# A three-block kernel: the modulation matrix read as row dot products, and six waits or orders around it changed

## The chip, the cores and the metric

The kernel runs on one core of one Trainium2 chip. The metric is the device time of one execution in microseconds (us), here the median of three runs.

## What is computed

Three transformer-like blocks, one after another, on one sequence of 1024 positions (T) with 1024 channels (D), all in float32. The parts that this change touches:

```python
# first block: gated linear recurrence in 4 heads of 128, computed in chunks
o = einsum('bhts,bhse->bhte', scores, vc) + einsum('bhtd,bhde->bhte', qc * exp(b), S)
# third block: six vectors of 1024 from each of two conditioning vectors
def ada_split(cond, w_ada, b_ada):              # w_ada: 1024 x 6144
    return jnp.split(jax.nn.silu(cond) @ w_ada + b_ada, 6, axis=-1)
sh1, sc1, g1, sh2, sc2, g2 = ada_split(c, w_ada, b_ada)
csh1, csc1, ... = ada_split(c_ctx, w_ada, b_ada)   # only csh1, csc1 are used
```

So the third block needs all 48 blocks of 128 numbers of silu(c) @ w_ada, and the first 16 of silu(c_ctx) @ w_ada. It also needs the layer norm of a context of 256 positions. Beside this each block has a mixer and a feed-forward network; the second block's network has the activation relu squared.

## The kernel before

The text calls the engines PE (TensorE, matmuls), DVE (VectorE), ACT (ScalarE), POOL (GpSimd) and SP (SyncE, which issues the transfers). The order of the work on each engine is written out by hand in one function per engine and stage, and engines wait for each other on semaphores. A float32 matrix product is made of three passes with rounded operands (`_r` tiles, a high and a low part each), so that nearly every product shows as three lines of PE in turn, as L2372, L2373, L2374. A stage ends with a barrier of all engines (`PEq L150` in the rows).

- **block1_mix** is the first block's mixer. For each of 4 heads its recurrence takes 1024 positions as 8 chunks of 128. `scores` (L405) makes a 128x128 product of keys and queries per chunk for each of several levels r, and DVE copies what the level's mask keeps (L740). Level 0 keeps, in each chunk, only keys of the first 64 and queries of the last 64 positions.
- **conv_stage** is the first block's feed-forward network, worked in pairs of hidden chunks, j = 0 to 12. A pair has seven products r in the manner of Strassen (`up`, L1317 to L1319) and a sweep of 16 units (n, m) over the outputs (`down`, L1328 to L1330), whose results DVE drains into the residual (L1761). ACT's `copy` (L1493) takes a finished sum out of PSUM, so that its bank comes free; `round_t` on ACT and `low_t` on DVE make the high and low part of the products' inputs; `low_part` (L1712, L1715) makes the low parts of the next pair's weights.
- **the attention block** (around L4400 to L5020) spills the residual X; its SP function ends with two transfers of 2 MB that bring X back, and a wait for them (`x_back`).
- **pair_stage** holds the end of the second block's mixer and its feed-forward network, in pairs i = 0 to 12 again. `up_pair(i)` is seven products r = 0 to 6 of 12 matmuls each (L2372 to L2374), `down_pair(i)` 16 units (n, m) of 6 matmuls (L2380 to L2382), drained by DVE (L2836). A matmul of 512 columns follows the last after 0.2265 us, as [rows 2] stand, so a pair is 180 matmuls. The products write PSUM banks 0, 1, 0, 2, 0, 2, 0: r = 6 needs the bank of r = 4, which DVE's `add(i, "22")` (L2822) frees. After r = 6, `down_pair` makes two sweeps of 12 matmuls over part of its inputs; the second needs the low part `low_y(i, "21")` (L2826), which needs `add(i, "21")` and then three ACT steps (L2575, L2577, L2579).
- **PairSide** puts the third block's conditioning beside these pairs. In i = 0 and 1 it takes the context's layer norm: parts q = 2i and 2i+1 are squared, added by DVE (`add_squares`, L2033) and summed over partitions by PE (`sums`, L2020). From i = 2 on it takes the modulation: 12 groups g of four blocks of 128 outputs. Group g is worked in pair i = g + 2, group 11 in the tail behind pair 12. A group is eight pieces k (128 inputs x 512 outputs, 256 KB each). DVE's `gemv(g, k)` multiplies piece k by the conditioning of those 128 inputs and adds it to an accumulator of 128x512 (L1985; L1988 for k = 0). For the four groups with both vectors a piece takes three such instructions (512, 256, 256). `sum_up` on PE (L2000) then adds the accumulator over partitions, one matmul of one column for each block (two rows of the profile each), and `keep` on ACT copies the result out. SP loads piece k+2 when `gemv(g, k)` is done, since there are two buffers (`rows`, `masks`).
- **the tail of pair_stage**: `load_tail(e)`, `round_tail`, `low_tail(j)` (L2855) and `down_tail(n, ms, e)` handle six last hidden chunks, e = 0 to 2, beside group 11.

In pair i = 3 to 12 DVE's order is gemv 0 to 2, add "11", low_down, low_y "11", gemv 3 to 5, add "22", gemv 6, add "21", low_y "22", gemv 7, low_y "21", low_y "12", and then 16 drains with the next pair's weight sums between them. In pair 2 the eight gemvs stand among the drains.

Of the kernel before, what the change touches and what calls it, by code (L numbers as in the profile page):

```python
# [38 lines left out]
def param_spec():  # L39
# [7 lines left out]
        ("c_3", 8), ("c_ctx_3", 8), ("b_ada_3", 48), ("ln_v_g_3", 4), ("ln_v_b_3", 4),  # L47
# [13 lines left out]
class Core:  # L61


    def __init__(self, nc, ctx, inputs, out):
# [37 lines left out]
        self.ctx_norm = nc.dram_tensor("ctx_norm", (P, KT * CTX), F32, kind="Internal").ap()  # L102
        self.row_copies = nc.dram_tensor("row_copies", (2, 8, T), F32, kind="Internal").ap()
# [123 lines left out]
def block1_mix(c, prefetch):  # L227
# [55 lines left out]
    with c.stage("products", "drained", "hi_ready", "lo_ready", "w_hi", "w_lo", "pieces", "masks_set", "bounds", "exps", "chain",  # L283
# [55 lines left out]
        def _(pe):  # L339
# [74 lines left out]
            def level(h, r):  # L414
                pe.wait_ge(w_ready, 9 * h + r + 1)
                pair_free(("level", h, r))
                scores(("level", h, r), Wl[r % 2], Wl[r % 2])
# [231 lines left out]
        def _(dve):  # L649
# [81 lines left out]
            def masks(what, r):  # L731
# [6 lines left out]
                s = pair_bank(what).rearrange("p a (b n) -> p (a b) n", n=CH)  # L738
                mask = c.ident[:, :].unsqueeze(1).to_broadcast([P, NC_, P]) if r is None else c.mask(r)
# [315 lines left out]
def counted(order):  # L1055
# [8 lines left out]
                  "ctx_scaled", "ada_a", "ada_b", "gemv", "summed", "ada_kept", "side_added")  # L1064
# [11 lines left out]
def conv_stage(c, w_out, up, down, first, last, mix_scale, alpha, follow, lead):  # L1076
# [99 lines left out]
    with c.stage(*names) as (block_, *sems):  # L1176
# [233 lines left out]
        def _(act):  # L1410
# [157 lines left out]
            gelu_early(2, 1)  # L1568
            round_t(3)
            for j in range(PAIRS):  # L1570
# [3 lines left out]
                copy(j, "11", 0)  # L1574
                if j:
                    gelu(j - 1)
                    if j < END:
                        round_part(j + 1, 0)
                    round_y(j - 1)
# [80 lines left out]
        def _(dve):  # L1660
# [200 lines left out]
            for j in range(PAIRS):  # L1861
# [15 lines left out]
                if j < END:  # L1877
                    low_part(j + 1, 4)
                    low_part(j + 1, 2)
                else:  # L1880
                    low_tail(0, w0)
                add(j, "21", 5)
                if j < END:
                    low_part(j + 1, 3)
                    for n in down_halves(j - 1):
                        for m in range(KT):
                            drain(j - 1, n, m)
                            if (n, m) == (0, 2):
                                low_part(j + 1, 5)
                            if (n, m) == (0, 5):  # L1890
                                low_part(j + 1, 6)
# [39 lines left out]
class PairSide:  # L1931

    GROUPS, BOTH, PART = 12, 4, 64
    ORDER = (4, 0, 1, 2, 3) + tuple(range(5, 12))

    def __init__(self, c):
# [3 lines left out]
        self.acc = [[c.rows[:, HALF:T]], [c.rows[:, T:TT], table[:, HALF:HALF + 256]]]  # L1940
# [4 lines left out]
        self.cond = c.small[:, 0:16].rearrange("p (k s) -> p k s", s=2)  # L1945
        self.ada = c.ada[:, :].rearrange("p (j s) -> p j s", s=2)
        self.done, at = {}, 0
        for g in range(self.GROUPS):
            for k in range(KT):
                at += 3 if self.both(g) else 1  # L1950
                self.done[g, k] = at

    def both(self, p):
        return self.ORDER[p] < self.BOTH

    def columns(self, p):
        return [(v, i) for v in range(2 if self.both(p) else 1) for i in range(HALF // P)]
# [9 lines left out]
    def load(self, sp, g, k):  # L1967
        at = self.ORDER[g] * P
        w = self.c.inp["w_ada_3"][at:at + P, k * HALF:(k + 1) * HALF]
        sp.dma_start(self.part[k % 2], w).then_inc((self.s["ada_a"], self.s["ada_b"])[k % 2], 16)  # L1970

    def gemv(self, dve, g, k):

        dve.wait_ge((self.s["ada_a"], self.s["ada_b"])[k % 2], 16 * (4 * g + k // 2 + 1))
        if k == 0 and g:
            dve.wait_ge(self.s["summed"], g)
        if k:
            dve.wait_ge(self.s["gemv"], self.done[g, k - 1])
        w = self.part[k % 2]
        for v in range(2 if self.both(g) else 1):  # L1980
            by, at = self.cond[:, k, v:v + 1], 0
            for acc in self.acc[v]:
                n = acc.shape[-1]
                if k:
                    dve.scalar_tensor_tensor(out=acc, in0=w[:, at:at + n], scalar=by, in1=acc, op0=ALU.mult,  # L1985
                                             op1=ALU.add).then_inc(self.s["gemv"], 1)
                else:
                    dve.tensor_scalar(acc, w[:, at:at + n], by, None, ALU.mult).then_inc(self.s["gemv"], 1)  # L1988
                at += n

    def sum_up(self, pe, g):
        pe.wait_ge(self.s["gemv"], self.done[g, KT - 1])
        if g:
            pe.wait_ge(self.s["ada_kept"], g)
        else:
            pe.wait_ge(self.s["ctx_log"], 4)
        n = len(self.columns(g))
        for j, (v, i) in enumerate(self.columns(g)):
            src = self.acc[0][0][:, i * P:(i + 1) * P] if v == 0 else self.acc[1][i // 2][:, (i % 2) * P:(i % 2 + 1) * P]
            mm = pe.matmul(self.c.PS[:, 3, j:j + 1], src, self.c.ones[:, 0:1], start=j == 0, stop=j == n - 1, skip_group_check=True)  # L2000
        mm.then_inc(self.s["summed"], 1)

    def keep(self, act, g):
        n, at = 2 if self.both(g) else 1, 4 * self.ORDER[g]
        act.wait_ge(self.s["summed"], g + 1)
        act.activation(self.ada[:, at:at + 4, 0:n], self.c.PS[:, 3, 0:4 * n].rearrange("p (s a) -> p a s", a=4),
                       ACT.Copy).then_inc(self.s["ada_kept"], 1)
# [8 lines left out]
    def sums(self, pe, q):  # L2016
        pe.wait_ge(self.s["side_added"], self.added(q) + 2)
        pe.wait_ge(self.s["ctx_centred"], 2 * (q // 2) + 2)
        out = self.c.PS[:, 3, self.PART * (2 + q % 2):self.PART * (3 + q % 2)]
# [4205 lines left out]
```

## Time and profile before

| | before |
|---|---|
| median of 3 runs | 3537.03 us (3535.54 to 3537.22) |
| the profiled execution | 3532.54 us, span 3530.8 us |
| TensorE's mean granted clock | 0.996 of full |
| busy: PE, DVE, ACT, POOL | 98%, 71%, 41%, 9% of the span |
| packets over the span | 331 MB, 94 GB/s |

The span is what lies between the first and the last instruction of one profiled execution; 1.7 us of its time lie outside. Its time is 4.5 us under the median. In a row of the timeline, the first number is the start within the span, the second how long the row took, xN how many instructions it stands for, and the bracket how long the engine had been idle and what released it.

### The profile page before, as it was taken

The numbers are of one execution on the slowest core, as the hardware profiler recorded it, in microseconds if no ns is written. First come the engines' busy times: TensorE is split into PE (matmuls) and PEld (weight loads), VectorE is DVE, ScalarE is ACT, GpSimd is POOL, SyncE is SP. The second block draws the span as 40 slices with busy tenths as digits, with TensorE's granted clock in tenths as the row PEclk, the third lists the DMA queues.
The fourth block names the chain that finished last, engine by engine and source line by source line (L and its number), as shares of the span: only waits on it lengthen the run. The fifth ranks groups of instructions, "written<-read, shape, count | busy, mean of one in ns | idle before, by whom it ended". The sixth has DMA issues, their size and how long they took to land. (4 is left out here: it accounts for less than half of the span.)

```text
span 3530.8 us, 42878 instructions
## 1 busy us (share of the span) xinstructions
PE 3448.1 (98%) x16610; PEld 2809.7 (80%) x16610; DVE 2519.2 (71%) x3472; ACT 1455.4 (41%) x2060; POOL 311.1 (9%) x313
## 2 busy tenths in 40 slices
PE   8999999999999999999999999999999999999998
PEld 7977877888887788667877888876987878888887
DVE  5387588888887798553567877656547587888895
ACT  3344363333345422542443333335423266772123
POOL 0000012222222001221000000003010000000000
PEclk9999999999999999999999999999999999999999
DMA  3102111111112113102223222331122214667651
GB/s 134 48 1 84 60 42 54 54 54 54 52 62 96 43 59 72 37 13 101 73 72 108 96 96 96 113 125 73 60 68 67 92 39 158 258 241 293 245 198 58
DMA packets 114526, 331.24 MB, mean 94 GB/s; under 512 B 18398, under 2 KB 33374, under 8 KB 105876
## 3 DMA queue, kind: packets, MB, share of 16 engines
q1 hardware_dynamic: 114324, 328.51, 26.7%
q8 instruction: 132, 2.16, 0.2%
q14 instruction: 70, 0.57, 0.1%
HBM read 253.82 MB, written 66.13 MB: 91 GB/s over the span
## 5 line engine op out<-in xcount | busy, mean ns | idle before, releaser
L2836 DVE TENSOR_TENSOR residual<-residual,psum 128x512 f32<-128x512 f32 x224 | 149.2, 683 | 57.1 <-PE psum L2382 56.9
L2380 PE MATMUL psum<-parts_r 128*128 128x512 f32 x448 | 177.3, 396 | 3.0 <-DVE parts_r L2855 1.5
L2382 PE MATMUL psum<-parts_r 128*128 128x512 f32 x448 | 174.9, 390 | 0.0
L2381 PE MATMUL psum<-parts_r 128*128 128x512 f32 x448 | 174.8, 390 | 0.0
L3872 DVE SCALAR_TENSOR_TENSOR residual<-psum,ada,residual 128x512 f32<-128x512 f32 x192 | 137.9, 746 | 38.0 <-PE psum L3426 19.8
L1763 DVE TENSOR_TENSOR residual<-residual,psum 128x512 f32<-128x512 f32 x256 | 160.1, 680 | 0.0
L4267 DVE SCALAR_TENSOR_TENSOR mixer<-scratch,params,mixer 128x1024 f32<-128x1024 f32 x120 | 156.9, 1307 | 4.0
L1317 PE MATMUL psum<-mixer_r,parts_r 128*128 128x512 f32 x304 | 118.3, 389 | 0.7 <-ACT rows L1440 0.7
L1318 PE MATMUL psum<-gemm_input_r,parts_r 128*128 128x512 f32 x304 | 118.3, 389 | 0.0
L1319 PE MATMUL psum<-mixer_r,parts_r 128*128 128x512 f32 x304 | 118.3, 389 | 0.0
L3568 ACT ACTIVATE parts_r<-parts 128x1792 fp32r<-128x1792 f32 x24 | 40.9, 1705 | 180.3 <-DVE parts L3856 180.3
L1328 PE MATMUL psum<-pairs_r 128*128 128x512 f32 x288 | 112.8, 392 | 2.0 <-DVE residual L1761 1.8
L358 PE MATMUL psum<-gemm_input_r,weights_r 128*128 128x512 f32 x256 | 105.3, 412 | 9.4 <-DVE residual_r L675 9.3
L1330 PE MATMUL psum<-pairs_r 128*128 128x512 f32 x288 | 112.1, 389 | 0.0
L1329 PE MATMUL psum<-pairs_r 128*128 128x512 f32 x288 | 112.1, 389 | 0.0
L1500 ACT ACTIVATE pairs<-pairs,params 128x1024 f32<-128x1024 f32 x36 | 42.9, 1239 | 142.8 <-PE psum L1330 142.8
L2380 PEld LDWEIGHTS psum<-parts_r 128*128 128x128 f32 x448 | 84.4, 188 | 21.4 <-DVE residual L2836 2.9
L360 PE MATMUL psum<-gemm_input_r,weights_r 128*128 128x512 f32 x256 | 100.4, 392 | 0.0
L359 PE MATMUL psum<-residual_r,weights_r 128*128 128x512 f32 x256 | 100.3, 392 | 0.0
L4887 DVE TENSOR_REDUCE small<-psum 128x1 f32<-128x512 f32 (+2 forms) x96 | 51.7, 555 | 67.0 <-PE psum L4598 65.8
L2382 PEld LDWEIGHTS psum<-parts_r 128*128 128x128 f32 x448 | 84.4, 188 | 17.8
L2381 PEld LDWEIGHTS psum<-parts_r 128*128 128x128 f32 x448 | 84.5, 189 | 17.0 <-issue 0.2
(961 smaller groups left out, 10773.6 us busy)
## 6 DMA issues: line engine op xcount, KB each, us to landing
y_blocks<-parts_r SPq DMA_DIRECT2D x84, 512.0 KB, 3.4
parts<-in_w SPq DMA_DIRECT2D x15, 1024.0 KB, 4.7
parts<-in_w_down SPq DMA_DIRECT2D x14, 1024.0 KB, 4.9
parts<-in_w_up SPq DMA_DIRECT2D x13, 1024.0 KB, 4.9
masks<-in_w_ada SPq DMA_DIRECT2D x48, 256.0 KB, 3.1
rows<-in_w_ada SPq DMA_DIRECT2D x48, 256.0 KB, 2.9
mixer_r<-y_blocks SPq DMA_DIRECT2D x12, 1024.0 KB, 9.6
low_r<-y_blocks SPq DMA_DIRECT2D x12, 1024.0 KB, 11.7
```

Source lines behind the costliest of these rows:

```text
L1317: pe.matmul(bank, a_high(place)[:, at], high[:, k, :], start=OPENS[r] and k == 0, stop=False, skip_group_check=True)
L1318: pe.matmul(bank, a_high(place)[:, at], low[:, k, :], start=False, stop=False, skip_group_check=True)
L1319: mm = pe.matmul(bank, a_low(place)[:, at], high[:, k, :], start=False, stop=k == 3, skip_group_check=True)
L1328: pe.matmul(bank, w_high[:, at], high, start=start, stop=False, skip_group_check=True)
L1329: pe.matmul(bank, w_low[:, at], high, start=False, stop=False, skip_group_check=True)
L1763: dve.tensor_tensor(x, x, ps, ALU.add).then_inc(drained, 1)
L2380: pe.matmul(bank, w_high[:, kd, at], high[:, 2 * kd + n, :], start=start, stop=False, skip_group_check=True)
L2381: pe.matmul(bank, w_low[:, kd, at], high[:, 2 * kd + n, :], start=False, stop=False, skip_group_check=True)
L2382: return pe.matmul(bank, w_high[:, kd, at], low[:, 2 * kd + n, :], start=False, stop=stop, skip_group_check=True)
L2836: dve.tensor_tensor(x, x, ps, ALU.add).then_inc(drained, 1)
L3872: dve.scalar_tensor_tensor(out=x, in0=ps, scalar=gate(m), in1=x, op0=ALU.mult, op1=ALU.add).then_inc(drained, 1)
L4267: dve.scalar_tensor_tensor(out=out, in0=U[:, j:j + T], scalar=w, in1=out, op0=ALU.mult, op1=ALU.add).then_inc(taps, 1)
```

## The change

Ten edits, in the kernel's order:

1. **Level 0 as a rectangle** (block1_mix): PE makes only the 64x64 part of each chunk that the mask keeps, and DVE copies it with a plain copy.
2. **copy(0, "11")** stands ahead of `round_t(3)` on ACT instead of behind it (conv_stage).
3. **low_part at j = 0** (conv_stage): three of five low parts move from before the drains to among them.
4. **x_back**: the attention stage no longer waits for X; DVE waits for it in pair_stage ahead of its first `mix_drain`.
5. **Context sums** in pair_stage, i = 0 and 1: `add_squares(q+1)` stands two units earlier, the next pair's `low_sums` one later.
6. **Modulation**: w_ada is laid out transposed. A piece is now one block of 128 outputs by 512 inputs; the first half of the inputs for all 48 blocks comes first, then the second half. One DVE instruction, `tensor_tensor_reduce`, multiplies a piece by a row of 512 silu values that is the same on all partitions and sums along the row into one column of `ada`, going on from what is there in the second half. Each waits for the one before. Where both vectors are wanted it is three instructions, and these pieces now alternate with single ones: groups 1 to 4 and 7 to 10 (pairs 3 to 6 and 9 to 12) have four of each kind, in place of four groups with eight.
7. `sum_up` and `keep` are gone.
8. **Conditions**: silu is taken of 16x128 numbers, stored to HBM, and read back as rows spread over all partitions, once for each half.
9. **Tail**: `low_tail(2)` and `(3)` stand ahead of gemv 4 to 7; `down_tail` takes all m at once for each e.
10. The context's normed values are loaded only when the last tail slab has landed.

```diff
 (level 0)
+                for i in range(NC_):
+                    keys, queries = ch(Wl[0], i)[:, 0:CH // 2], ch(Wl[0], i)[:, CH // 2:CH]
+                    mm = pe.matmul(chunk_of(("level", h, r), i)[0:CH // 2, CH // 2:CH], keys, queries, ...)
+                if r == 0:
+                    dve.tensor_copy(far, s[0:CH // 2, :, CH // 2:CH]).then_inc(masked, 1)
+                    return
 (conv_stage, ACT)
+            copy(0, "11", 0)
             round_t(3)
 (conv_stage, DVE)
+                        lows = {(0, 1): 4, (0, 3): 2, (0, 5): 3, (0, 6): 5, (0, 7): 6}
 (PairSide)
-    ORDER = (4, 0, 1, 2, 3) + tuple(range(5, 12))
+    ORDER = tuple(range(32, 40)) + tuple(b for j in range(16) for b in (j, 16 + j)) + tuple(range(40, 48))
+        dve.wait_ge(self.s["gemv"], at)
+        dve.tensor_tensor_reduce(out=self.c.PS[:, 3, :] if kept else w[:, j * n:(j + 1) * n],
+                                 in0=w[:, j * n:(j + 1) * n], in1=by, scale=1.0,
+                                 scalar=out if half or j else 0.0, op0=ALU.mult, op1=ALU.add, accum_out=out)
-                        elif side is not None and (n, m) == (1 if i == 2 else 0, 6):
-                            side.sum_up(pe, i - 2)
-                side.keep(act, i - 2)
 (pair_stage, SP)
+                sp.wait_ge(*tail_landed[2 * EARLY - 2])
+                sp.wait_ge(*tail_landed[2 * EARLY - 1])
                 sp.dma_start(c.PW[:, 8:10, :], c.ctx_norm...)
 (pair_stage, DVE)
-                        if i < END and (n, m) == (1, 3):
+                        if i < END and (n, m) == (1, 4 if side is not None and i < 2 else 3):
                             low_sums(i + 1)
-                        if contexts and (n, m) == (1, 4):
+                        if contexts and (n, m) == (1, 2):
                             side.add_squares(dve, q + 1)
 (attention stage, SP)
-            sp.wait_ge(x_back, 32)
```

The order on DVE in pair 3 between its fourth product's add and its low parts, before: gemv 5 (three instructions), add "22", gemv 6 (three), add "21", low_y "22".

```order
L1985 SCALAR_TENSOR_TENSOR rows<-masks,small,rows 128x512
L1985 SCALAR_TENSOR_TENSOR rows<-masks,small,rows 128x256
L1985 SCALAR_TENSOR_TENSOR masks<-masks,small 128x256
L2822 TENSOR_TENSOR parts<-parts,psum 128x512
L2826 TENSOR_TENSOR parts_r<-parts,parts_r 128x512
```

The same place of the change, where a dot product stands as two rows, ISA with its elements and ISA 128x1, the read-out of its sum: gemv 5 (single), add "22", gemv 6 (both), add "21", low_y "22".

```order
L2020 ISA rows,ada<-rows 128x512
L2020 ISA ada 128x1
L2833 TENSOR_TENSOR parts<-parts,psum 128x512
L2020 ISA psum,ada<-masks,rows 128x512
L2020 ISA ada 128x1
L2020 ISA masks,ada<-masks,rows 128x256
L2020 ISA ada 128x1
L2020 ISA masks,ada<-masks,ada 128x256
L2020 ISA ada 128x1
L2833 TENSOR_TENSOR parts<-parts,psum 128x512
L2837 TENSOR_TENSOR parts_r<-parts,parts_r 128x512
```

So ahead of add "22" three instructions became one with a read-out, and ahead of add "21" three became three with read-outs.

The order on DVE in pair 0 from unit (1, 0) on, before (L2033 is `add_squares`, L2808 `low_sums`, L2836 a drain):

```order
L2836 TENSOR_TENSOR residual<-residual,psum 128x512
L2033 TENSOR_REDUCE rows<-rows 128x64
L2836 TENSOR_TENSOR residual<-residual,psum 128x512
L2804 TENSOR_TENSOR parts_r<-parts,parts_r 128x1024
L2836 TENSOR_TENSOR residual<-residual,psum 128x512 x2
L2808 TENSOR_TENSOR parts_r<-parts,parts_r 128x2560
L2836 TENSOR_TENSOR residual<-residual,psum 128x512
L2033 TENSOR_REDUCE rows<-rows 128x64
```

and of the change, whose lines are L2847, L2050, L2815 and L2819 for the same four:

```order
L2847 TENSOR_TENSOR residual<-residual,psum 128x512
L2050 TENSOR_REDUCE rows<-rows 128x64
L2847 TENSOR_TENSOR residual<-residual,psum 128x512
L2815 TENSOR_TENSOR parts_r<-parts,parts_r 128x1024
L2847 TENSOR_TENSOR residual<-residual,psum 128x512
L2050 TENSOR_REDUCE rows<-rows 128x64
L2847 TENSOR_TENSOR residual<-residual,psum 128x512 x2
L2819 TENSOR_TENSOR parts_r<-parts,parts_r 128x2560
```

The second reduction now stands ahead of the long `low_sums` instead of behind it.

The order on DVE in conv_stage at j = 0, before (L1712 and L1715 are `low_part`, L1727 an add, L1761 a drain):

```order
L1712 TENSOR_TENSOR parts_r<-rows,parts_r 128x1024
L1715 TENSOR_TENSOR parts_r<-parts,parts_r 128x512 x2
L1727 TENSOR_TENSOR pairs<-pairs,psum 128x512
L1715 TENSOR_TENSOR parts_r<-masks,parts_r 128x512
L1761 SCALAR_TENSOR_TENSOR residual<-residual,psum 128x512 x3
```

and of the change (L1725, L1728, L1740 and L1774 for the same):

```order
L1725 TENSOR_TENSOR parts_r<-rows,parts_r 128x1024
L1740 TENSOR_TENSOR pairs<-pairs,psum 128x512
L1774 SCALAR_TENSOR_TENSOR residual<-residual,psum 128x512 x2
L1728 TENSOR_TENSOR parts_r<-parts,parts_r 128x512
L1774 SCALAR_TENSOR_TENSOR residual<-residual,psum 128x512 x2
L1728 TENSOR_TENSOR parts_r<-parts,parts_r 128x512
```

The first drains now stand behind one short add, and the low parts between drains.

## Rows read from the trace of the kernel before

**Rows 1.** The page, busy time of each engine.

```profile
PE 3448.1 (98%) x16610; PEld 2809.7 (80%) x16610; DVE 2519.2 (71%) x3472; ACT 1455.4 (41%) x2060; POOL 311.1 (9%) x313
```

**Rows 2.** Timeline of PE in pair 5.

```profile
2010.38 0.50 PE L2372 MATMUL psum<-mixer_r,parts_r 128*128 128x512 f32 x1 [0.89 <-DVE parts L2822]
2010.71 0.40 PE L2373 MATMUL psum<-low_r,parts_r 128*128 128x512 f32 x1
...
2022.75 1.39 PE L2000 MATMUL psum<-ones,rows 128*128 128x1 f32 x12
...
2024.45 0.48 PE L2380 MATMUL psum<-parts_r 128*128 128x512 f32 x1
```

**Rows 3.** Groups by line on PE, pairs 3 to 6 (busy, mean ns | idle before).

```profile
L2372 PE MATMUL psum<-mixer_r,parts_r 128*128 128x512 f32 x75 | 29.7, 395 | 3.6 <-DVE parts L2822 3.6
```

**Rows 4.** Groups by line and shape on DVE.

```profile
L1985 DVE SCALAR_TENSOR_TENSOR rows<-rows,small 128x512 f32<-128x512 f32 x48 | 35.9, 749 | 19.7 <-DMA rows<-in_w_ada 18.3
...
L1985 DVE SCALAR_TENSOR_TENSOR rows<-rows,small 128x256 f32<-128x256 f32 x16 | 7.6, 478 | 0.0
...
L2072 DVE TENSOR_TENSOR ada<-ada,params 128x32 f32<-128x32 f32 x1 | 0.2, 186 | 0.0
...
L702 DVE TENSOR_TENSOR_SCAN mixer<-scratch 128x1024 f32<-128x1024 f32 x4 | 8.8, 2272 | 0.7 <-issue 0.7
...
L740 DVE COPY_PREDICATED norm_b<-masks,psum 128x1024 f32<-128x1024 int32 x28 | 36.5, 1303 | 4.2 <-PE psum L405 4.1
...
L4904 DVE COPY gemm_input<-psum 64x512 f32<-64x512 f32 x15 | 10.2, 682 | 0.2
```

**Rows 5.** Timeline of DVE in pair 5.

```profile
1998.97 0.75 DVE L1985 SCALAR_TENSOR_TENSOR rows<-masks,small,rows 128x512 f32<-128x512 f32 x1 [2.52 <-DMA masks<-in_w_ada]
...
2003.83 0.74 DVE L1985 SCALAR_TENSOR_TENSOR rows<-rows,small 128x512 f32<-128x512 f32 x1
...
2005.47 0.75 DVE L1985 SCALAR_TENSOR_TENSOR rows<-masks,small,rows 128x512 f32<-128x512 f32 x1
...
2008.18 0.75 DVE L1985 SCALAR_TENSOR_TENSOR rows<-rows,small 128x512 f32<-128x512 f32 x1 [1.17 <-DMA rows<-in_w_ada]
...
2009.64 0.68 DVE L2822 TENSOR_TENSOR parts<-parts,psum 128x512 f32<-128x512 f32 x1
...
2011.69 0.68 DVE L2822 TENSOR_TENSOR parts<-parts,psum 128x512 f32<-128x512 f32 x1
...
2014.41 0.69 DVE L2826 TENSOR_TENSOR parts_r<-parts,parts_r 128x512 fp32r<-128x512 f32 x1
```

**Rows 6.** Timeline of PE, whole span, rows with a wait.

```profile
185.15 2.05 PE L405 MATMUL psum<-scratch 128*128 128x128 f32 x16 [0.16 <-DVE scratch L729]
...
522.29 0.47 PE L1317 MATMUL psum<-low_r,parts_r 128*128 128x512 f32 x1 [1.81 <-ACT pairs L1493]
...
540.66 0.50 PE L1328 MATMUL psum<-pairs_r 128*128 128x512 f32 x1 [1.81 <-DVE residual L1761]
...
1606.71 0.47 PE L2326 MATMUL psum<-mixer_r,pairs_r 128*128 128x512 f32 x1 [2.67 <-PEq L150]
...
1813.51 0.43 PE L2020 MATMUL psum<-rows,ones_d 128*128 128x64 f32 x2 [1.89 <-DVE rows L2033]
...
1857.64 0.47 PE L2020 MATMUL psum<-rows,ones_d 128*128 128x64 f32 x2 [1.85 <-DVE rows L2033]
...
1903.77 0.50 PE L2380 MATMUL psum<-parts_r 128*128 128x512 f32 x1 [0.89 <-DVE residual L2836]
...
2341.14 0.50 PE L2380 MATMUL psum<-gemm_input_r,low_r 128*128 128x512 f32 x1 [0.83 <-DVE mid_r L2855]
...
2353.20 0.50 PE L2380 MATMUL psum<-parts_r 128*128 128x512 f32 x1 [1.46 <-DVE parts_r L2855]
...
2411.86 0.67 PE L943 MATMUL psum<-mixer,ones_d 128*128 128x512 f32 x1 [1.06 <-PEq L150]
```

**Rows 7.** Transfers issued from 2338 to 2352 us, median us to landing.

```profile
pairs<-ctx_norm SPq DMA_DIRECT2D x1, 1024.0 KB, 11.1
```

More of the change, by code:

```diff
@@ L1949, in __init__, with chunk, both @@
             for k in range(KT):
-                at += 3 if self.both(g) else 1
+                at += 3 if self.both(g, k) else 1
                 self.done[g, k] = at
[L1953 to L1957, printed above, removed]
+    def chunk(self, g, k):
+        half, at = divmod(KT * g + k, self.BLOCKS)
+        return half, self.ORDER[at]
+    def both(self, g, k):
+        return self.chunk(g, k)[1] < self.BOTH
     def load_part(self, sp, q, j):
@@ L1972, in gemv @@
     def gemv(self, dve, g, k):
+        half, block = self.chunk(g, k)
         dve.wait_ge((self.s["ada_a"], self.s["ada_b"])[k % 2], 16 * (4 * g + k // 2 + 1))
[L1975 to L2007, printed above, removed]
+        if (KT * g + k) % self.BLOCKS == 0:
+            dve.wait_ge(self.s["cond_moved"], 32 + 48 * (half + 1))
+        w, at = self.part[k % 2], self.done[g, k] - (3 if self.both(g, k) else 1)
@@ new lines, in gemv @@
+        for v in range(2 if self.both(g, k) else 1):
+            out = self.ada[:, block, v:v + 1]
+            for j, by in enumerate(self.by[v]):
+                n = by.shape[-1]
+                if at:
+                    dve.wait_ge(self.s["gemv"], at)
+                at += 1
+                kept = v == 0 and self.both(g, k)
+                dve.tensor_tensor_reduce(out=self.c.PS[:, 3, :] if kept else w[:, j * n:(j + 1) * n], in0=w[:, j * n:(j + 1) * n], in1=by, scale=1.0,
+                                         scalar=out if half or j else 0.0, op0=ALU.mult, op1=ALU.add,
+                                         accum_out=out).then_inc(self.s["gemv"], 1)
@@ L2477, in _ @@
                 down_pair(i)
-            if side is not None:
-                for e in TAIL:
-                    down_tail(0, range(0, 7), e)
-                    if e == 1:
-                        side.sum_up(pe, END - 1)
-                pe.wait_ge(s["ada_kept"], END)
-                for e in TAIL:
-                    down_tail(0, range(7, KT), e)
-            else:
-                for e in TAIL:
-                    down_tail(0, range(KT), e)
+            for e in TAIL:
+                down_tail(0, range(KT), e)
             if follow is None:
@@ L2940, in _ @@
                 low_t(r)
-            if side is not None:
-                dve.wait_ge(s["cond_ready"], 2)
             for i in range(PAIRS):
@@ L2993, in _ @@
                     side.scale(dve, q + 1)
-            for j in (2, 3):
-                low_tail(j)
-                if side is not None:
-                    for k in (2 * j, 2 * j + 1):
-                        side.gemv(dve, END - 1, k)
+            low_tail(2)
+            low_tail(3)
+            if side is not None:
+                for k in range(4, 8):
+                    side.gemv(dve, END - 1, k)
             low_tail(4)
```

89 lines of the change are left out of this document (59 added, 30 removed).

## Prediction, made before the changed kernel ran

> **What bounds the kernel now.** I read the page first. PE is busy for 98% of the span, DVE for 71% [rows 1]. The reader is to see that only two things can shorten this kernel: fewer rows on PE, or fewer waits of PE. DVE has time over in the mean, but where PE waits it is nearly always for DVE. So the next view was PE's timeline, every row with a bracket. PE is not busy for 3530.8 - 3448.1 = 82.7 us in all, spread over some eighty places, so each edit must be costed at its own place.
>
> What a wait costs is more than its bracket. In pair 5 the row of r = 6 has 0.89 in its bracket, but it starts 1.05 us later than the rhythm of 0.2265, and the row after it follows after 0.33 instead of 0.23 [rows 2]. So I add 0.16 to every bracket, and 0.1 for the slow start: 0.26 in all.
>
> **The modulation in pairs 3 to 12.** A pair's 180 matmuls take 180 x 0.2265 = 40.77 us. The sixteen rows of `sum_up` in a pair with both vectors start at 2022.75 and the next unit at 2024.45 [rows 2], which with a slow start is 1.80; by half, 0.90 where one vector is wanted. Four pairs have 1.80 and six have 0.90 (the tail is costed below): 12.6 us of PE rows that go. In the four pairs with both, r = 6 also waits for add "22", 3.6 us of brackets in all [rows 3], 4.6 with 4 x 0.26. If nothing took their place, 17.2 us would be won here.
>
> What takes their place is DVE's price of a dot product. No row of this trace has one. A multiply-add of 128x512 takes 0.749, one of 256 columns 0.478; a tiny operation takes 0.186 [rows 4]. Each dot product is an instruction over the piece, then a read-out of the sum, and each waits for the one before. The low bound is that the read-out hides: 0.75 and 0.48. Above it: 0.69, a plain copy's or product's time, plus 0.19 is 0.88 for 512 columns, and (0.42 + 0.19) 0.61 for 256. A high value puts two tiny operations behind it, one for the read-out and one for the semaphore: 1.06 and 0.80. The farthest row is the scan, a running sum at 2.272 us for 1024 columns [rows 4]; by its slope and with the same two behind it, 1.5 and 0.94. I take 0.88 and 0.61, nearest to the instructions that do the same arithmetic. A piece with both is then 2.10 (before, 1.45 from 2008.18 to 2009.64) and a single one 0.88.
>
> Pair 5 by its rows [rows 5]. Piece 2 (both) starts at 1998.97 as before, since its transfer decides; it takes 0.65 more, so gemv 3 starts at 2004.5 instead of 2003.83 and, single now, is over at 2005.4. Gemv 4 (both) is over at 2007.5. Piece 5 is asked for after gemv 3 and lands 2.7 later (2005.47 to 2008.18 in the rows): 2008.1. Gemv 5 (single) is over at 2009.0, where it was 2009.64. Add "22" starts then, and r = 6 0.74 behind it (2009.64 to 2010.38 in the rows): 2009.74. PE's rhythm would have it start at 2010.38 - 1.05 = 2009.33, so it is 0.4 late, where it was 1.05. Behind add "22" stands gemv 6 (both), whose piece lands at 2010.2, so it is over at 2012.3, and add "21" follows 0.6 later than its 2011.69. Low_y "21" comes 2.72 after it (ACT's three steps lie between): 2015.0, and PE can take the second sweep at 2015.7. PE has 24 matmuls before it and arrives at 2009.74 + 0.1 + 5.44 = 2015.3, so it waits 0.4. That is the next thing to be late. With 0.1 for each start it makes 1.0 us in a mixed pair, and there are eight of them, not four: 8 us. In the two single pairs nothing is late, since each piece adds 0.03 to 0.14. So 17.2 - 8 = **9.2 us less**. At the low bound no wait is left: 17.2 less. At 1.06 and 0.80 the same steps give waits of 1.3 and 1.35, 2.8 in a pair, 22.6 in all: 5.4 more. At 1.5 and 0.94 they give 3.5 and 1.7, 5.4 in a pair, 43 in all: 26 more.
>
> A rule speaks against this edit. The row first: the multiply-add with two float32 operands in SBUF takes 0.749 for 512 columns against 0.68 for a plain copy of 512 [rows 4], so it runs at full rate; but it gives out no sum. The Trainium skill (Vector Engine (DVE) Microarchitecture Reference, section 7, Points that are easy to get wrong) says that this family of instructions with two SBUF sources that aren't bf16 runs at half rate, as no read port is left for the accumulator. The row denies it for the form without a sum; for the form with one nothing here decides. By the rule the sum would be that of the farthest bound, by the row the one taken.
>
> **Pair 2** has its gemvs among the drains, two at a time, and DVE is late there: PE waits 0.89 at 1903.77 [rows 6] just behind `sum_up`. What `sum_up` gives back is therefore lost in that wait, and the eight dot products cost 8 x 0.13 more, of which their transfers hide about half: **0.5 more** (0 to 1.5).
>
> **The other edits** [rows 6].
> - Level 0: 16 rows of 128x128 start at 185.15 and take 2.05, in a rhythm near 0.11. At 64 columns anything from nothing to half of the 1.8 may go; I take 0.3, as a matmul of one column has the same rhythm (16 in 1.70, [rows 2]). DVE's masked copy of 128x1024 is 1.30, the plain 64x512 one 0.68 [rows 4]; PE waits for DVE in this stage at many places (the first is the row at 185.15), so I count half of the 0.62. Together 0.6 in each of four heads, **2.5 less** (1.0 to 4.3: the upper end has the whole 0.62 and 0.45).
> - conv_stage: PE waits 1.81 for ACT's copy at 522.29. ACT does it behind `round_t(3)`; ahead of it, the most that can go is 2.07. But r = 3 needs the low part of that `round_t(3)`, which now starts a copy later, so I take 0.75. At 540.66 PE waits 1.81 for the first drain, which stands behind three low parts; one short add is left ahead of it. The most is again 2.07; as the low parts among the drains now hold those up, I take about half, 1.15. Together **1.9 less** (0.8 to 3.5).
> - x_back: PE starts 2.67 us after the barrier row at 1606.71; at a stage end that nothing else delays it is 1.06 (2411.86). **1.6 less** (1.0 to 2.1). X is first touched by `mix_drain`, behind a whole unit of matmuls, which covers the landing.
> - Context sums: PE waits 1.89 and 1.85 for the reduction, 4.1 with 0.16 each. It stands behind the long `low_sums`; ahead of it nothing is late. **4.0 less** (3.0 to 4.1). What stands behind, `low_sums`, is needed only by the next pair, four units on.
> - Tail: PE waits 0.83 (2341.14) and 1.46 (2353.20), and the last `sum_up` of 0.9 goes. The first wait goes with the order. The last slab is asked for later by one `low_tail`, because gemv 5 is; but the context's 1 MB no longer shares the queue with it (it takes 11.1 us there [rows 7]), and e = 2 is wanted 12 matmuls later. I take the second wait as it is: **1.9 less** (0.5 to 3).
> - The condition rows cost three small transfers, twice, on SP, most of a pair ahead of their use, and one wait for a store ahead of the context's loads, which a whole half pair hides. Nothing; with that cover gone, a transfer of 2 to 3 us once (a piece takes 2.7).
>
> **The sum**: 9.2 - 0.5 + 2.5 + 1.9 + 1.6 + 4.0 + 1.9 = 20.6 us less than the profiled 3532.5. That execution is 4.5 under the median, and I take the same step from the median: 3537.0 - 20.6 = 3516.4.
>
> **The rivals.**
> - *The read-out hides* (0.12). For it: the read-out moves one number for each partition. Against it: each dot product waits on the last. 8 us more than forecast: 3508.
> - *The read-out is dear, near 1.06* (0.16). Two waits in each of eight mixed pairs, 2.8 us a pair, eat more than the won 17.2, and the rest of the edits is left with 11.4 - 5.4 = 6 less, 3531. About half of it is within 0.2%.
> - *Half rate* (0.12), the other side: DVE is 3.5 late at r = 6 and 1.7 at the second sweep in eight pairs, 26 more; pair 2 and the tail add about 3 (eight dot products each, 0.6 dearer, half of it covered). Less the 11.4 of the other edits: 17 more, 3554. It turns slower where a mixed pair waits over (17.2 + 11.4)/8 = 3.6 us, near 1.2 us for 512 columns. The Trainium skill's rule of above leads here.
> - *The other waits only change place* (0.12): the next input is as late at r = 3, among the low parts, and at the stage's end. Then of 11.4 about 4 stays: 3524. For it, each of these waits has another input close behind; against it, the order has the longer operation behind the wanted one at each.
> - The forecast as worked out has 0.48, and 3511 to 3523 as its own range.
>
> **The numbers.** 0.2% is 7 us, about what a measurement of this kernel can tell from no change. Faster by more: 0.48 + 0.12 + half of the dear case + 0.08 of the last = 0.76. Within: 0.08 + 0.04 = 0.12. Slower: 0.12. The range goes from 3506, just under the low bound of the read-out, to 3536, past the dear case; it leaves out the half rate and little else.
>
> **What would show it.** The dot product's row and the start of the next: 0.85 to 0.95 apart for 512. In the eight mixed pairs, r = 6 with brackets under 0.5 and a wait for low_y (L2837) at the second sweep under 0.5 too; a mixed pair near 41.8, a single one 40.8. No rows of `sum_up`. The brackets at 1813 and 1857 gone, that at the attention block's end near 1. Wrong would be: brackets over 1 at both places in each mixed pair (dear or half rate), or PE waiting in pair 2 by more than 2 us.

## The result

| | before | changed |
|---|---|---|
| median | 3537.11 us (3535.54 to 3537.22, 4 runs) | 3504.72 us (3503.69 to 3506.18, 4 runs) |
| profiled execution, span | 3532.54, 3530.8 | 3506.18, 3504.5 |

The ratio is 0.9911 (0.9899 to 0.9924): 32 us faster, where 20.6 was forecast. The time lies 1.3 us under the low end of the range. The direction was right, and the forecast gain a third and more too small.

The changed kernel's page, busy time and granted clock:

```profile
PE 3436.9 (98%) x16482; PEld 2796.2 (80%) x16482; DVE 2519.9 (72%) x3632; ACT 1454.5 (42%) x2047; POOL 312.8 (9%) x313
...
PEclk9999999999999999999999999999999999999999
```

PE has 11 us less to do than in [rows 1] and 128 instructions fewer, the rows of `sum_up`. DVE's busy time is the same in all, though not because the dot products are as cheap: their rows, read-outs included, sum to 114 us, those of the multiply-adds to about 96. The clock digits don't tell the two kernels apart, and yet part of the result is in the clock, as shown below.

**Where the time went, place by place.** The way to read two traces of one kernel is to follow the shift of the same matmul. Three of before (the first after the first mixer, the first of a norm behind conv_stage, one in the mixer's end):

```profile
348.64 0.47 PE L1269 MATMUL psum<-mixer_r,pairs_r 128*128 128x512 f32 x1 [0.59 <-PEq L150]
...
1124.37 0.70 PE L943 MATMUL psum<-norm_b,ones_d 128*128 128x512 f32 x1 [0.74 <-POOL norm_b L965]
...
1711.17 0.47 PE L2326 MATMUL psum<-mixer_r,pairs_r 128*128 128x512 f32 x1 [0.74 <-ACT mixer L2542]
```

and the same three of the changed kernel, with the first behind the attention block between them:

```profile
346.95 0.47 PE L1281 MATMUL psum<-mixer_r,pairs_r 128*128 128x512 f32 x1 [0.30 <-PEq L151]
...
1121.03 0.70 PE L955 MATMUL psum<-norm_b,ones_d 128*128 128x512 f32 x1 [0.71 <-POOL norm_b L977]
...
1601.02 0.47 PE L2352 MATMUL psum<-mixer_r,pairs_r 128*128 128x512 f32 x1 [0.70 <-PEq L151]
...
1705.46 0.47 PE L2352 MATMUL psum<-mixer_r,pairs_r 128*128 128x512 f32 x1 [0.75 <-ACT mixer L2557]
```

The shift, the time by which the changed kernel reaches the same matmul earlier, is 1.7 us at the first (level 0), 3.3 at the second (conv_stage 1.7 more) and 5.7 at the last. The row at 1601.02 answers to 1606.71 in [rows 6]: its bracket fell from 2.67 to 0.70, which is 2.0 of the last step of 2.4.

The pairs, as the distance between the first matmuls of two pairs, in the changed kernel:

```profile
1973.56 0.39 PE L2398 MATMUL psum<-mixer_r,parts_r 128*128 128x512 f32 x1
...
2014.80 0.39 PE L2398 MATMUL psum<-mixer_r,parts_r 128*128 128x512 f32 x1
...
2055.60 0.39 PE L2398 MATMUL psum<-mixer_r,parts_r 128*128 128x512 f32 x1
```

Pair 5, a mixed one (four pieces with both vectors, four single), takes 41.24 us, with a start 0.3 late at r = 4. Pair 6 takes 40.80, which is 180 matmuls and nothing else. Pairs 3 to 6 took 44.17, 43.55, 43.80 and 43.65 before, the single ones 41.70. From pair 3 to the start of the last pair, the sum of the distances went from 383.67 to 367.81. With the last pair's own `sum_up` (0.9) that is **16.8 us less**, where 9.2 was forecast. No bracket at all is left on r = 6.

The waits that stay or are new, PE's timeline of the changed kernel:

```profile
522.64 0.47 PE L1329 MATMUL psum<-mixer_r,parts_r 128*128 128x512 f32 x1 [1.09 <-DVE gemm_input_r L1734]
...
542.29 0.50 PE L1340 MATMUL psum<-pairs_r 128*128 128x512 f32 x1 [0.22 <-DVE residual L1774]
...
1890.46 0.50 PE L2406 MATMUL psum<-parts_r 128*128 128x512 f32 x1 [1.67 <-DVE residual L2847]
...
2325.28 0.50 PE L2406 MATMUL psum<-parts_r 128*128 128x512 f32 x1 [2.77 <-DVE parts_r L2866]
```

Conv_stage has 1.09 at r = 3 and small ones of 0.2 among the drains, as forecast. Pair 2 waits 1.67 at one unit, where [rows 6] had 0.89 and `sum_up` ahead of it. The tail's wait is 2.77 where it was 1.46 in this pair of traces (more of it below). Those at 1813.51 and 1857.64 are gone.

### The profile page after: what moved, and what is told of

Read it like the earlier page. It is cut to its first block and busy times, and to the rows that moved or that the text cites. A ratio compares the mean times of both kernels' runs of the same rounds, so it can differ in the third digit from the quotient of the medians.

```text
span 3504.5 us, 42764 instructions
## 1 busy us (share of the span) xinstructions
PE 3436.9 (98%) x16482; PEld 2796.2 (80%) x16482; DVE 2519.9 (72%) x3632; ACT 1454.5 (42%) x2047; POOL 312.8 (9%) x313
## 5 line engine op out<-in xcount | busy, mean ns | idle before, releaser
L2847 DVE TENSOR_TENSOR residual<-residual,psum 128x512 f32<-128x512 f32 x224 | 145.6, 681 | 41.1 <-PE psum L2408 40.0
```

Source lines behind the costliest of these rows:

```text
L2847: dve.tensor_tensor(x, x, ps, ALU.add).then_inc(drained, 1)
```

## The experiments

**Modulation alone.** The kernel before with edits 6 to 8 of the list alone; the tail keeps its order, without `sum_up`.

```diff
-                    if e == 1:
-                        side.sum_up(pe, END - 1)
-                pe.wait_ge(s["ada_kept"], END)
```

> The kernel before with the modulation's edits alone (row dot products, alternating pieces, condition rows, no sum_up and keep); the tail keeps its order and its split of m, and all other edits are left out. Theory A, the gain is the sum of waits and PE rows that the two traces show place by place: pairs 3 to 12 16.8 us less, pair 2 0.4, pair 0 1.9 because the context's loads now go out behind the store of the conditions: 19 less than before, near 3518. Theory B, a part of the 32 us between the medians comes from stretches at half clock that change from run to run and with the waits: then less or more than 19 by over 3 us, with as many such stretches in the trace. In both, pairs 3 to 12 are 40.8 us each.

3517.97 us, ratio 0.9946 (0.9933 to 0.9958): 19 less, as theory A has it. Its pairs 3 to 11 take 40.80 each except one of 41.25. But the reason given for the 1.9 us of pair 0 was wrong (below), so that the sum of theory A is right to the microsecond only by luck; the interval is 4 us wide to either side. Three waits of it on PE:

```profile
1816.10 0.44 PE L2023 MATMUL psum<-rows,ones_d 128*128 128x64 f32 x2 [1.85 <-DVE rows L2036]
...
1904.88 0.50 PE L2390 MATMUL psum<-parts_r 128*128 128x512 f32 x1 [1.66 <-DVE residual L2837]
...
2336.96 0.50 PE L2390 MATMUL psum<-parts_r 128*128 128x512 f32 x1 [1.63 <-DVE parts_r L2856]
```

The first is the context's, which this version still has. The second shows that pair 2's 1.66 belongs to the modulation.

**The other edits alone.** Level 0, conv_stage, x_landed and the context sums.

```diff
-                        if i < END and (n, m) == (1, 3):
+                        if i < END and (n, m) == (1, 4 if side is not None and i < 2 else 3):
```

> The kernel before with level 0 as a rectangle, the two edits of conv_stage, x_landed and the context sums; modulation and tail as before. Theory A: 2.1 + 1.7 + 1.9 + 4.1 = 9.8 less, near 3527, and the wait at the third product of pair 0 (1.61 in the bracket) stays, since it belongs to the condition rows. If that wait is gone too, it belongs to one of these edits. Theory B: off by over 3 us.

3525.28 us, ratio 0.9971 (0.9960 to 0.9983): 10 by the ratio, 12 by the medians. The four waits at r = 6 are there as before (1.27, 0.50, 1.42 and 0.45), the first of them:

```profile
1911.78 0.50 PE L2388 MATMUL psum<-mixer_r,parts_r 128*128 128x512 f32 x1 [1.27 <-DVE parts L2838]
```

The two halves make 19 + 10 = 29 by the ratios, 32 by the medians, and the whole change 31.5 and 32: within the noise nothing is lost or won between them. The tail's edits are in neither half and were not run alone; their worth is read from traces below. The wait at the third product of pair 0 was gone here as well, with the ctx loads in their old place. So the claim that the condition rows remove it was wrong.

**Both pieces together.**

```diff
-    ORDER = tuple(range(32, 40)) + tuple(b for j in range(16) for b in (j, 16 + j)) + tuple(range(40, 48))
+    ORDER = tuple(range(32, 40)) + tuple(range(32)) + tuple(range(40, 48))
```

> The changed kernel with the pieces of both vectors in four whole groups (pairs 3, 4, 9 and 10) instead of every second piece of eight. If the alternation is what keeps DVE in time: r = 6 waits about 1.5 us in each of these four pairs, 6 us more than the changed kernel, near 3511. Rival: the dot products are cheap enough in any order, and the time stays within 2 us of the changed kernel's 3504.7.

3509.73 us, 5 over the changed kernel. The first and the last of four such waits at r = 6:

```profile
1911.50 0.50 PE L2398 MATMUL psum<-mixer_r,parts_r 128*128 128x512 f32 x1 [1.49 <-DVE parts L2833]
...
2201.61 0.50 PE L2398 MATMUL psum<-mixer_r,parts_r 128*128 128x512 f32 x1 [1.24 <-DVE parts L2833]
```

The four brackets are 1.49, 1.14, 1.18 and 1.24. So the alternation is worth 5 to 6 us of the 17; the rest is the matmuls of `sum_up`. With three instructions in every piece DVE is as late at add "22" as before the change, and a little more.

**Earlier slab and pieces.**

```diff
-                    for k in range(6):
+                    for k in range(2):
                         sp.wait_ge(s["gemv"], side.done[END - 1, k])
                         side.load(sp, END - 1, k + 2)
                     sp.wait_ge(products, downs_done(END))
                 load_tail(e)
+                (the pieces of k = 2 to 5 behind it)
-    GEMVS_BESIDE = {(0, 1): range(0, 2), (0, 4): range(2, 4), (0, 7): range(4, 6), (1, 2): range(6, 8)}
+    GEMVS_BESIDE = {(0, 1): range(2, 4), (0, 4): range(4, 6), (0, 7): range(6, 8)}   # 0, 1 ahead of add "22"
```

> The changed kernel with two orders moved: the last tail slab is asked for behind the second gemv of the tail instead of the sixth, and pair 2 takes its first two gemvs ahead of add 22 instead of among the drains. If the late slab makes the wait of 2.77 us at the end of the tail and the half clock behind it: both go, 2.9 + 1.4 less, and pair 2 loses 1.5 of its wait of 1.67: near 3499. Rival: the slab shares the queue with the last pieces and is no sooner, or gemv 6 and 7 then hold up its low part: no gain.

3501.73 us, 3 less than the changed kernel instead of the 5 to 6 expected; the intervals of their ratios overlap (0.9886 to 0.9917 here). Its waits in pair 2 and in the tail:

```profile
1875.48 0.50 PE L2410 MATMUL psum<-parts_r 128*128 128x512 f32 x1 [0.82 <-DVE residual L2851]
...
1891.16 0.50 PE L2410 MATMUL psum<-parts_r 128*128 128x512 f32 x1 [0.54 <-DVE residual L2851]
...
2323.68 0.50 PE L2410 MATMUL psum<-parts_r 128*128 128x512 f32 x1 [0.48 <-DVE parts_r L2870]
```

The tail's went from 2.77 to 0.48. Pair 2 won 1.1 at its last wait and lost 0.82 at a new one: pieces 2 and 3 now stand on SP behind the next pair's 1 MB of weights and land late.

**Before again, and dearer dots.** The second has one tiny copy behind each dot product:

```diff
+                dve.wait_ge(self.s["gemv"], at)
+                dve.tensor_copy(self.c.small[:, at % 64:at % 64 + 1], self.c.ones[:, 0:1])
```

> The kernel before, word for word, for a second trace of it. The wait of 1.61 us at the third product of pair 0 was gone both with the modulation alone and without it, so no edit owns it: if it is the jitter of one transfer, this trace has no such wait there and the transfer of hidden_rows lands 6.1 us after its issue, not 7.9. If it is there again, both experiments removed it, each in its way. At r = 6 of pairs 3 to 6 the waits of 0.7 to 1.3 stay in any case.

> The changed kernel with one tiny copy behind every dot product, which waits for it, so that a piece with both vectors takes about 2.2 us to the next instruction and a single one 0.94: near the 2.10 and 0.88 with which the prediction counted. If only that price was wrong, its steps now come true: waits of 0.4 at r = 6 and 0.4 at the second sweep in the eight mixed pairs, 8 us more than the changed kernel, near 3513. If the steps themselves leave out some slack, the waits are smaller and the time is under 3509.

Before again, one execution: 3540.61 us, 8 over the first profiled one. The wait of 1.61 in pair 0 isn't there, so it was the jitter of a transfer: the stores of `hidden_rows` landed 7.9 us after their issue in the trace with the wait and 6.4 here. The changed kernel shows 1.23 there in one of its four traces, too, with 7.5, and no wait in the others, with 6.0 to 6.2. Dearer dots: 3510.35 us, 5.6 over the changed kernel, between the two outcomes named (3513 and under 3509). DVE and PE of it:

```profile
1981.34 0.70 DVE L2020 CUSTOM_DVE_ANT_0 psum<-masks,rows 128x512 f32<-128x512 f32 x1 [2.19 <-DMA masks<-in_w_ada]
...
1983.34 0.69 DVE L2835 TENSOR_TENSOR parts<-parts,psum 128x512 f32<-128x512 f32 x1
...
1915.32 0.50 PE L2408 MATMUL psum<-parts_r 128*128 128x512 f32 x1 [0.28 <-DVE parts_r L2839]
...
2233.50 0.50 PE L2400 MATMUL psum<-mid_r,parts_r 128*128 128x512 f32 x1 [0.62 <-ACT parts L2583]
```

A piece with both vectors takes 2.00 to the add behind it (1981.34 to 1983.34), where the forecast had 2.10. Yet the brackets on PE are 0.28 and 0.62 in two of eight mixed pairs; the others have starts 0.1 to 0.3 late. The excess of pairs 3 to 11, seven of them mixed, over 40.80 sums to 3.8 us, and 0.6 of it the changed kernel has, too: about 0.5 for each mixed pair. The prediction's steps had 1.0 at 2.10 and 0.88. Worked again with the prices of this trace, 2.00 and 0.81 (1990.10 to the add at 1990.91), they give about 0.7, an estimate. So the steps were somewhat too dear, too. And 0.62, the longest of the waits, stands at r = 4, a place that the steps left out.

**Earlier slab alone, and late gemvs.** The first edit of above alone; then with it the last two gemvs of pair 2 at (1, 5):

```diff
-    (0, 7): range(4, 6), (1, 2): range(6, 8)}
+    (0, 7): range(4, 6), (1, 5): range(6, 8)}
```

> The changed kernel with the last tail slab asked for behind the second gemv of the tail, and nothing else moved. All that the version with both orders won came from here: the same 3502 within 1.5. If the pieces moved in pair 2 gave something too, this one is over 3503.

> The same, and in pair 2 the last two gemvs behind the long low part (1, 5) instead of ahead of it (1, 2). If those two are what makes PE wait 1.67 there, the wait falls to under 0.4 and the time is 1.3 to 1.8 under that of the slab alone. Rival: gemv 0 and 1 of pair 3 then start late by the transfer of their pieces, and r = 6 of pair 3 waits instead.

The slab alone: 3499.59 us. That is 2 under the version with both orders, more than the 1.5 expected; by the ratios (0.9900 and 0.9901) the two are the same, so the moved pieces of pair 2 gave nothing. With late gemvs: 3503.81. Here the rival came true, at r = 4 of pair 3 where it was named at r = 6. Pair 2 fell to 42.49 us, but pair 3 rose to 45.86. DVE and PE of pair 3:

```profile
1899.35 0.70 DVE L2020 CUSTOM_DVE_ANT_0 psum<-masks,rows 128x512 f32<-128x512 f32 x1 [3.50 <-DMA masks<-in_w_ada]
...
1901.03 0.68 DVE L2837 TENSOR_TENSOR parts<-parts,psum 128x512 f32<-128x512 f32 x1
...
1904.23 0.50 PE L2402 MATMUL psum<-mid_r,parts_r 128*128 128x512 f32 x1 [3.15 <-ACT parts L2585]
```

Piece 2 now stands on SP behind 1 MB of `w_down` and lands 3.5 us after DVE is ready for it. Add "11" (1901.03) comes late by it, then ACT's steps and its copy, and PE waits 3.15 at r = 4, the fifth product. PE then ran at full clock for about 1 us and fell to half:

```profile
core 0: us, PE busy (x), PEclk, DMA share, GB/s
1905.60:1908.60 3.00, 3.00 (x9) 0.50 0.49 120
```

**Long and short waits.** Sums that nobody reads, ahead of add "22" in pairs 3 to 12 (two and five in the short version):

```diff
+                    for _ in range(7 if i in (7, 8) else 4):
+                        dve.reduce_sum(c.small[:, (7 * i + _) % 64:(7 * i + _) % 64 + 1], c.par[:, 0:512], AX_X)
```

> The changed kernel with four (in the two single pairs seven) sums over 512 constants of 0.6 us each ahead of add 22 in pairs 3 to 12, read by nobody. PE must then wait for about 1.8 us (single: 2.4) at r = 6 of each of ten pairs: 20 to 22 us in the trace. Theory C: the stretches at half clock that all traces show begin just behind waits of this size, so about a third of the ten has one, 1.4 to 1.6 us each, the mean clock falls, and the time is 25 us or more over the changed kernel's 3504.7: 3530 or over. Rival: such stretches come at any place; then two or three in all, and 3525 to 3527.

> The same with two (single: five) such sums: waits of about 0.6 (1.2) at r = 6, 7 to 9 us in the trace, 3512 to 3514. Theory C: no half clock behind these, the mean clock as in the changed kernel. Rival: as many such stretches as behind the long waits.

Long: 3523.49 us, under the 3525 to 3527 of the rival; the ten brackets go from 1.17 to 2.93 and sum to 15.8. The time rose by 18.8 over the changed kernel's first median and by 19.7 over that on the same chip (below). Short: 3510.59, under the 3512 to 3514 expected; its brackets are 0.4 and less in the mixed pairs, 0.83 and 1.55 in the single ones, and none is followed by half clock. The two longest brackets of the long version, and the granted clock behind the longest:

```profile
2082.57 0.50 PE L2398 MATMUL psum<-mixer_r,parts_r 128*128 128x512 f32 x1 [1.97 <-DVE parts L2833]
...
2126.64 0.50 PE L2398 MATMUL psum<-mixer_r,parts_r 128*128 128x512 f32 x1 [2.93 <-DVE parts L2833]
```

```profile
core 0: us, PE busy (x), PEclk, DMA share, GB/s
2126.70:2130.70 4.00, 4.00 (x18) 1.00 0.02 2
```

Not one of the ten is followed by half clock. Theory C, that waits of this size bring it, falls as it was stated. The 0.26 that the prediction added to each bracket is a little short: in eight of the nine pairs 3 to 11 the pair's excess over 40.80 is 0.30 to 0.34 more than the bracket (the ninth, pair 5, has its late start at r = 4 besides).

**The two versions side by side.** No edit.

> The changed kernel, word for word, on the chip of the next run, for the comparison with it: 3504.7 within 2, and a tail wait that varies with the landing of the last slab.

> The changed kernel with the earlier slab alone, word for word as before, on the same chip as the changed kernel. If it is better: 3 to 5 us less than that one, with a tail wait under 0.5 where the changed kernel has 1.9 to 2.8. Rival: the two differed by the clock of their runs alone, and are within 1.5.

3503.82 against 3500.25 us on the same chip: the earlier slab is 3.6 better (ratios to before 0.9905 and 0.9896, whose intervals overlap), with no bracket of 0.2 or more in this trace's tail. It is the best version found, in both of its comparisons.

**Four more traces.** No edit; two of before, two of the changed kernel.

> The kernel before again, for a third trace. If it loses more to half clock than the changed kernel, the stretches sum to 4 to 8 us as in the second trace and part of them stand at the edited places (near 541, 1818, 1862 or 2357); if not, they sum to 2 to 4 as in the changed kernel's traces.

> The changed kernel again, for a third trace: stretches at half clock of 3 to 4 us in all, none near the five places whose waits went.

> A fourth trace of the kernel before, with the same question as the third.

> A fourth trace of the changed kernel, with the same question as its third.

With the first traces and the repeats there are four of each. For each, the span was cut into windows of 4 us, and in those in which PE worked and the granted clock was under 0.99, one minus the clock was multiplied by the length. The sum is called clock loss here. It is an estimate: a window in which PE also waits counts in full.

| trace | span | clock loss | of it at edited places |
|---|---|---|---|
| before 1 to 4 | 3530.8, 3538.9, 3532.5, 3536.5 | 10.4, 22.4, 15.0, 21.2 | 1.7, 5.1, 5.1, 3.4 |
| changed 1 to 4 | 3504.5, 3502.3, 3502.2, 3501.3 | 15.4, 12.0, 15.9, 12.8 | 1.7, 0, 0, 0 |
| mean before, changed | 3534.7, 3502.6 | 17.3, 14.0 | 3.8, 0.4 |

The spans differ by 32.1 us in the mean, and without the clock loss by 28.9. The clock loss differs by 3.2, and the edited places alone by 3.4 (near 541, 1816, 1858 and 2352 of before; 2326 of the changed kernel). Such a stretch in before's first trace, and one in the changed kernel's tail beside one in attention that every trace has, as windows of PE:

```profile
core 0: us, PE busy (x), PEclk, DMA share, GB/s
1856.00:1858.00 2.00, 0.36 (x3) 0.98 0.00 0
1858.40:1861.40 3.00, 3.00 (x9) 0.51 0.03 5
```

```profile
core 0: us, PE busy (x), PEclk, DMA share, GB/s
2326.30:2329.30 3.00, 3.00 (x8) 0.50 0.55 175
1430.00:1434.00 4.00, 3.86 (x11) 0.50 0.01 2
```

0.51 and 0.50 of 2.4 GHz is the level of 1.2 GHz. Two starts in the third trace of before behind which it fell:

```profile
541.70 0.64 PE L1328 MATMUL psum<-pairs_r 128*128 128x512 f32 x1 [1.81 <-DVE residual L1761]
...
2352.36 0.79 PE L2380 MATMUL psum<-parts_r 128*128 128x512 f32 x1 [3.21 <-DVE parts_r L2855]
```

## Why the prediction fell short

- **The modulation in pairs 3 to 12: the mechanism was right, and the term that was mis-sized is "so 17.2 - 8 = 9.2 us less".** It measured 16.8. What the rows of `sum_up` and the old waits were worth (17.2) was right; the 8 us of new waits never came. The step that failed is the price, "I take 0.88 and 0.61": a piece with both vectors cost 1.67 us, not 2.10, and a single one ahead of an add 0.62, not 0.88. Groups by line of DVE, the changed kernel:

```profile
L2020 DVE CUSTOM_DVE_ANT_0 rows<-rows,ada 128x512 f32<-128x512 f32 x24 | 18.0, 749 | 6.8 <-DMA rows<-in_w_ada 5.8
...
L2020 DVE CUSTOM_DVE_ANT_0 rows<-rows 128x512 f32<-128x512 f32 x24 | 16.5, 689 | 5.7 <-DMA rows<-in_w_ada 4.6
...
L2020 DVE CUSTOM_DVE_ANT_0 masks<-masks,ada 128x256 f32<-128x256 f32 x32 | 15.5, 485 | 1.1
...
L2020 DVE DVE_READ_ACCUMULATOR2_ANT ada<- 128x1 f32 x160 | 15.0, 94 | 0.0
```

The main instruction takes 0.69 in the first half of the inputs, 0.75 in the second, and the read-out 0.09. DVE's timeline of pair 5, which answers to [rows 5]:

```profile
1979.86 0.70 DVE L2020 CUSTOM_DVE_ANT_0 psum<-masks,rows 128x512 f32<-128x512 f32 x1 [2.90 <-DMA masks<-in_w_ada]
...
1981.53 0.68 DVE L2833 TENSOR_TENSOR parts<-parts,psum 128x512 f32<-128x512 f32 x1
...
1984.93 0.68 DVE L2020 CUSTOM_DVE_ANT_0 rows<-rows 128x512 f32<-128x512 f32 x1
...
1985.77 0.70 DVE L2020 CUSTOM_DVE_ANT_0 psum<-masks,rows 128x512 f32<-128x512 f32 x1
...
1988.15 0.69 DVE L2020 CUSTOM_DVE_ANT_0 rows<-rows 128x512 f32<-128x512 f32 x1 [0.63 <-DMA rows<-in_w_ada]
...
1988.77 0.09 DVE L2020 DVE_READ_ACCUMULATOR2_ANT ada<- 128x1 f32 x1
1988.77 0.68 DVE L2833 TENSOR_TENSOR parts<-parts,psum 128x512 f32<-128x512 f32 x1
...
1990.03 0.70 DVE L2020 CUSTOM_DVE_ANT_0 psum<-masks,rows 128x512 f32<-128x512 f32 x1 [0.58 <-DMA masks<-in_w_ada]
...
1991.71 0.68 DVE L2833 TENSOR_TENSOR parts<-parts,psum 128x512 f32<-128x512 f32 x1
```

A single dot product is followed by a waiting one after 0.84 (1984.93 to 1985.77), near the forecast; but an instruction that doesn't need its sum follows after 0.62, with the read-out beside it (add "22", 1988.15 to 1988.77). The three of a mixed piece take 1.67 to the add, not 2.10, since the 256-column ones follow each other after 0.46 rather than 0.61. The two adds that PE waits for stand behind just such ends of pieces: add "22" came 15.2 us into the pair, not 16.0, and add "21" 18.2, not 19.3. The rival "the read-out hides" described this case, with 0.12 and 3508. The rival "the other waits only change place" did not come: it left 4 of the 11.4 us of the other edits, and about 12 stayed.
- **Its steps were a little too dear as well.** At nearly the assumed price, the dearer dots have 0.5 us a mixed pair where the steps, worked with their prices, have 0.7. In eight pairs that is some 2 us, an estimate; the price made the rest of the 8. Which step has the slack, no run separates.
- **Half rate** did not come. From 256 to 512 columns a dot product grows from 0.485 to 0.749, by 0.26 us, and the multiply-add of [rows 4] by 0.27: the sum costs the instruction no rate. The Trainium skill's sentence (Vector Engine (DVE) Microarchitecture Reference, section 7, Points that are easy to get wrong) on two SBUF sources that aren't bf16 did not come true here, for either form. It names the scalar_tensor_tensor family; the trace has this instruction as CUSTOM_DVE_ANT_0, and no run shows whether the sentence is meant to cover it. That the output goes to PSUM in the mixed pieces changes it by 0.01 (0.698 and 0.758).
- **Pair 2**: forecast 0.5 more; 44.07 us in the mean of four traces against 44.42 before: 0.3 less. That `sum_up`'s 0.9 is lost to the drains was right.
- **Level 0** 1.7 to 2.1 against 2.5; **conv_stage** 1.7 against 1.9; **x_back** 2.0 against 1.6; **context sums**: both brackets gone, 4.1 against 4.0. All in their ranges, with the next waits where they were named.
- **Tail**: 1.9 forecast. The first two traces alone would say 0.7, as the last wait grew from 1.46 to 2.77. The four of each say otherwise: 1.46, 2.42, 3.21 and 2.51 before, 2.77, 1.97, 0.85 and 1.86 after, so 2.4 and 1.9 in the mean. With the first wait (0.8 with its start) and the last `sum_up` (0.9) that makes 2.3 less. The slab's landing sets this wait: in the four traces of the changed kernel its 1 MB of `hidden_rows` landed 8.6, 8.0, 7.0 and 8.0 us after its issue, in the order of the waits, and asked for earlier it leaves 0.5 and less. One trace was a poor base for it.
- **The sum** of the measured terms is 16.8 + 1.9 + 1.7 + 2.0 + 4.1 + 2.3 = 28.8, beside the 28.9 that the means of four traces have without the clock loss. That they agree to 0.1 is chance: pair 2's 0.3 is left out, and level 0 is a mean of 1.7 to 2.1.
- **The base.** The forecast took one trace's steps from the median. That trace of before was a quick one: it had 10.4 us of clock loss, where the four have 17.3 in the mean. The edits took away waits behind which PE sometimes fell to half clock, 3.2 us in the mean, and no term stood for it. This is the second step that failed, a term put at nothing. 28.8 alone would have ended inside the range, at 3508.

What stays open: why half clock follows some of the removed waits in conv_stage, at the context sums and in the tail (8 of the 20 in before's four traces have it within 3 us), and the 3.15 at r = 4 with the late gemvs, but none of ten artificial waits of up to 2.93 at r = 6. Nothing that was tried tells these places apart. That the removed waits caused the half clock behind them is read from four traces of each kernel and not shown by an experiment.

## What to carry to other kernels

Price a read-out or a semaphore by who needs it: the next instruction on the same engine that doesn't read the result starts as if it were not there, and a critical add behind the end of such a chain gains that much. Spread the dear pieces over more stages when the stage, and not the sum, sets the wait: here that was worth 5 to 6 us with the same work in all. Ask in which order the transfers stand on the queue before moving a consumer: two of three moved orders here were lost to a 1 MB transfer that came to stand ahead. And take two or three traces of the kernel before as the base, when the sum of the terms is under one per cent.

## What the hardware showed that was not expected

PE's clock drops to 0.50 in every trace: near 1430 us for some 10 us, at the end of the span, and for 3 to 4 us each at some other places, which differ from execution to execution. 10 to 22 us are lost so in a span of 3500. The slower executions of before are those with more of it (granted clock 0.995 to 0.996 at 3530 to 3533 us, 0.992 to 0.994 at 3537 to 3541), but it is not all of their spread: without the clock loss the four spans of before still lie 5 us apart, and one of them has the transfer that landed late. The clock fell behind some waits of 1.8 to 3.2 us and not behind ten others of 1.2 to 2.9.
